# The rounding of a weight unit moved from ahead of a projection's successor to right behind the projection

## The chip, the cores and the metric

The kernel runs on one core of a Trainium2 chip. Its time is device microseconds of that core. Three runs of the kernel before took 1092.4 to 1093.69 us, median 1093.59.

The core's engines work side by side, each through its own list of instructions in order: TensorE (PE in the profile; its weight loads are PEld), VectorE (DVE), ScalarE (ACT), GpSimd (POOL) and SyncE (SP, which here only starts transfers). They wait for each other through semaphores.

## The reference

Batch 1, 256 positions, width 1024, float32. One block of three mixers and two more layers:

```python
h = rms_norm(x, norm1_g[l]);  u = h @ w_in[l]        # 1024 -> D_IN
(dq, dk, dv, iq, ik, iw, nq, nkv, ng, sz, sxbc, sdt, mg) = jnp.split(u, offsets, axis=-1)
y_a = dsa_mixer(...)     # indexed attention, 16 heads
y_b = nsa_mixer(...)     # compressed, selected and window attention, 16 heads
y_c = ssd_mixer(...)     # state space mixer: causal conv, scan by chunks, norm
mix = g0 * (y_a @ w_br_dsa[l]) + g1 * (y_b @ w_br_nsa[l]) + g2 * (y_c @ w_br_ssd[l])
x = x + mix @ w_out[l]
x = x + jnp.square(jax.nn.relu(rms_norm(x, norm2_g[l]) @ w_ff1[l])) @ w_ff2[l]
```

Then an even layer (`even_mixer`: a gated, 31-tap convolved and layer-normed half `ya`, and a multi-scale pooled half `yb`, joined by an output projection), an odd layer (`odd_mixer`: a 4-tap convolution, two gates by small per-head products, a linear recurrence over time, a gate, an output projection), each added to x, and a last norm. Everything is a matrix product of a normed activation by a weight, and elementwise work and recurrences around it.

## The kernel before

**Weights.** All projection weights come as one stream of 286 units of 512 KB (eight blocks of 128 x 128 float32), in the order in which they are used, into a ring of five places (`RING`, SyncE, from L603). Products are made in a split form: a weight W is rounded to fp32r, W_hi, and the rest, W_lo = W - W_hi, is kept beside it; so is each activation. For each block TensorE makes three products of 128 x 256: W_hi by x_hi, W_hi by x_lo, W_lo by x_hi (L1794, L1795, L1796). The weights of `b_val` and `pool` (`PLAIN`) are taken in one product (L1779), without splitting; the other 276 units are split.

**A step `wsplit`** of unit u is two instructions. ScalarE writes W_hi into one of three places (`ring_hi`, `HIS` = 3; L897), when the transfer has landed and TensorE is through with the split unit three before (L896). GpSimd or VectorE then subtracts (`remainder`, L562): the function `on_gpsimd` gives 182 units to GpSimd (all of dq, nq, br_dsa, val_glu, b_gate, a_gate, even_yb, xr, gate, two in three of xbc, half of others) and 94 to VectorE. TensorE waits for the remainder before a unit's first block.

**Jobs.** A job is one output block of 128 channels of one projection: `PHASES` lists each projection with its number of jobs and the blocks in each. Most have 8 blocks, one unit a job; `pool` has 2, `odd_out` 12, `br_ssd` 16, `ff2` 32. A job writes one of three PSUM slots and its reader frees it.

**Order.** `schedule()` writes one list of steps by hand, and each engine walks this list in order and issues its share of every step. There is no planner. A job step is TensorE's matmuls and, on ScalarE or VectorE, the reading of its PSUM slot (L981 on, L1007, L1012, L1030). Behind a job stand the steps that go with it; here they are called its epilogue: `split` (rounding L918 or L920 and remainder L570 or L1140 of a finished activation, for a later projection), `sA` to `sR` (softmax), `xconv` (L1361, the convolution, which frees the PSUM slot of xbc), `uA`, `uE`, `uB`, `ysq`, `ysum` (state space), `econv` (L1432), `winsum` (L731 to L735, on GpSimd), `gact`, `scan` and others. For the eight jobs of the head (`HEAD`: iq twice, ik, dk, kc, vc, ks, kw) and the first six of val_glu (`LATE`), the input's norm is not known when TensorE starts; ScalarE reads their slots only when VectorE has scaled them in place (step `scale`, L1147), a step behind the next job.

The `wsplit` of unit u stands directly ahead of the job in which unit u-2 begins (`AHEAD` = 2). Between two jobs a and b the list thus reads: job a, a's epilogue, `wsplit` of the unit two ahead, job b. Places that come up below: br_dsa 0 reads the split outputs of the DSA attention, whose last `split` steps stand behind mg 23; even_yb 0 reads the splits of yb, behind the last pool jobs; even_ya 0 reads those of ya, behind even_yb 7.

The code around the change, with what calls it:

Of the kernel before, what the change touches and what calls it, by code (L numbers as in the profile page):

```python
# [40 lines left out]
for _name, _w in COLUMNS:  # L41
# [5 lines left out]
PHASES = [("iq", 2, 8), ("ik", 1, 8), ("dk", 1, 8), ("kc", 1, 8), ("vc", 1, 8), ("ks", 1, 8), ("kw", 1, 8),  # L47
          ("dq", 8, 8), ("nq", 8, 8), ("xbc", 24, 8), ("sz", 16, 8), ("mg", 24, 8),
          ("br_dsa", 8, 8), ("br_nsa", 8, 8), ("br_ssd", 8, 16), ("w_out", 8, 8),
          ("ff1", 32, 8), ("ff2", 8, 32), ("val_glu", 16, 8), ("b_val", 8, 8), ("b_gate", 8, 8),  # L50
          ("a_gate", 8, 8), ("pool", 8, 2), ("even_yb", 8, 8), ("even_ya", 8, 8), ("xr", 12, 8), ("gate", 12, 8),
          ("odd_out", 8, 12)]
# [38 lines left out]
def schedule():  # L91
# [128 lines left out]
    order = first + a_gate + jobs["b_gate"] + pool  # L220
# [71 lines left out]
    at, splits = 0, {}  # L292
    order = [s for s in out if s[0] == "job"]
# [4 lines left out]
    for u in range(units):  # L298
        if starts[8 * u][1] not in PLAIN:
            splits.setdefault(("units", u) if u < AHEAD else starts[8 * (u - AHEAD)], []).append(("wsplit", u))  # L300
    final = []
    for s in out:
        final += splits.get(s, []) + [s]
    out = final
    assert len(set(out)) == len(out)
    return out
# [44 lines left out]

def program(nc, x_t, w_stream, w_tok, w_cmp, w_rgi, cols, rows, out):
    steps = schedule()
    where, turns = psum_tenants(steps)
    slots = {"proj": 3, "score": 2, "turn": 1, "pv": 1, "mean": 1}
# [1523 lines left out]
```

How the kernel before makes its waits and increments, by code:

```python
        def readers_done(eng, key):  # L502
            g, n = where[key]
            prev = n - slots[g]
            if prev >= 0:
                for e in turns[g][prev]:
                    eng.wait_ge(read[g, e], sum(e in r for r in turns[g][:prev + 1]))
# [1 line left out]
        def was_read(eng, key, reader="A"):  # L510
            g, n = where[key]
            eng.wait_ge(read[g, reader], sum(reader in r for r in turns[g][:n + 1]))
# [45 lines left out]
        def remainder(eng, u):  # L559
            eng.wait_ge(sem("w_hi_ready"), hi_turn[u])
            return eng.tensor_tensor(ring_lo[:, u % RING, :, :].rearrange("p k n -> p (k n)"),
                                     ring[:, u % RING, :, :].rearrange("p k n -> p (k n)"),
                                     ring_hi[:, hi_slot[u], :, :].rearrange("p k n -> p (k n)").bitcast(F32),
                                     ALU.subtract)
# [1 line left out]
        def part_remainder(eng, tag, c):  # L567
            src, hi, lo, _, _ = parts[tag]
            eng.wait_ge(sem(f"hi_{tag}"), c + 1)
            return eng.tensor_tensor(lo(c), src(c), hi(c).bitcast(F32), ALU.subtract)
# [21 lines left out]
        @block.sync  # L592
# [8 lines left out]
                    sp_eng.dma_start(wcmp, w_cmp).then_inc(sem("wcmp_in"), 16)  # L601
                if u >= RING:
                    sp_eng.wait_ge(filled["proj"], used[u - RING])
                if u == first["job", "even_ya", 5] // 8:
                    sp_eng.wait_ge(sem("yaf_ready"), 8)
                    sp_eng.dma_start(flat(WG, 12), w_rgi).then_inc(sem("wrgi_in"), 16)
```

## Time and profile before

| | |
|---|---|
| median of three runs | 1093.59 us (1092.4 to 1093.69) |
| the profiled execution | 1093.34 us |
| its span, first instruction to last | 1091.6 us, 21399 instructions |
| TensorE busy | 1050.3 us, 96%, 8185 matmuls |
| VectorE, ScalarE, GpSimd busy | 704.0, 594.9, 602.4 us |
| HBM read | 155.65 MB |

1.7 us of the profiled execution lie around its span. All times in the rows are microseconds from the start of the span, except where a row says ns. A busy time counts an engine as busy from the start of an instruction to its end; for TensorE neighbouring matmuls overlap, so their mean is longer than their spacing.

### The profile page before, as it was taken

The page shows a single profiled execution, that of the slowest core. Times are in us where ns is not written, and L with a number is a line of the kernel's source. Part 1 is how long each engine was busy: PE and PEld are TensorE (multiplying, and loading weights), DVE is VectorE, ACT ScalarE, POOL GpSimd, SP SyncE. Part 2 cuts the span into 40 slices and gives each one's busy share as a digit, 9 for nine tenths or more (in the row PEclk, how much of TensorE's full clock was granted, in tenths as well). Part 3 has the DMA queues.
Part 4 walks back from the last instruction along what each step waited for, and adds up shares of the span by engine and source line. Part 5 has one row for each costly group of instructions (what it writes and reads, how often), then busy time and mean ns, then how long its engine had stood idle before and what let it go on. Part 6 is the DMA issues. An engine that isn't in the chain of part 4 may idle for free.

```text
span 1091.6 us, 21399 instructions
## 1 busy us (share of the span) xinstructions
PE 1050.3 (96%) x8185; PEld 986.2 (90%) x8185; DVE 704.0 (64%) x1479; ACT 594.9 (54%) x1193; POOL 602.4 (55%) x454
## 2 busy tenths in 40 slices
PE   9999999999999999999999999999999989999986
PEld 8799878998889999889999999999898978899986
DVE  7869676666663325785485553333898967588974
ACT  5454667667664457764445554335333447368742
POOL 3656445444444469545534334337678857466951
PEclk9999999999999999999999999999999999999999
DMA  8234333333224443225545555555444534544442
GB/s 314 96 123 143 117 104 110 116 117 116 97 98 136 136 135 98 97 97 175 183 164 177 190 177 187 180 175 174 155 157 145 182 125 145 194 138 153 152 144 72
DMA packets 43157, 158.08 MB, mean 145 GB/s; under 512 B 4912, under 2 KB 4912, under 8 KB 42672
## 3 DMA queue, kind: packets, MB, share of 16 engines
q1 hardware_dynamic: 42912, 156.69, 43.0%
q8 instruction: 65, 1.06, 0.4%
q14 instruction: 36, 0.29, 0.1%
q10 hardware_dynamic: 144, 0.03, 0.0%
HBM read 155.65 MB, written 1.05 MB: 144 GB/s over the span
## 4 chain that ended last, share of the span: by engine, by line
PE 75%; DVE 14%; ACT 5%; POOL 3%; issue 2%; DMA 0%; DVEq 0%; SPq 0%; ACTq 0%; POOLq 0%
PE p_proj L1794 20%; PE p_proj L1795 19%; PE p_proj L1796 19%; PE p_score L1632 3%; PE p_proj L1779 3%; PE p_pv L1660 2%; POOL ring_lo L562 2%; ACT ring_hi L897 1%; PE p_turn L1642 1%; DVE ring_lo L562 1%; PE p_mean L1541 1%; PE p_score L1552 1%; DVE arena L1361 1%; PE p_score L1700 1%; POOL arena_r L570 1%
## 5 line engine op out<-in xcount | busy, mean ns | idle before, releaser
L1794 PE MATMUL p_proj<-arena_r,ring_hi 128*128 128x256 f32 x2208 | 657.7, 298 | 15.7 <-POOL ring_lo L562 6.5
L1795 PE MATMUL p_proj<-arena_r,ring_hi 128*128 128x256 f32 x2208 | 625.6, 283 | 0.0
L1796 PE MATMUL p_proj<-arena_r,ring_lo 128*128 128x256 f32 x2208 | 625.5, 283 | 0.0
L562 POOL TENSOR_TENSOR ring_lo<-ring,ring_hi 128x1024 fp32r<-128x1024 f32 x182 | 437.8, 2407 | 287.5 <-ACT ring_hi L897 286.7
L1794 PEld LDWEIGHTS p_proj<-arena_r,ring_hi 128*128 128x128 f32 x2208 | 423.7, 192 | 35.1 <-issue 19.9
L1795 PEld LDWEIGHTS p_proj<-arena_r,ring_hi 128*128 128x128 f32 x2208 | 424.2, 192 | 8.1 <-issue 6.0
L1796 PEld LDWEIGHTS p_proj<-arena_r,ring_lo 128*128 128x128 f32 x2208 | 423.9, 192 | 0.0
L897 ACT ACTIVATE ring_hi<-ring 128x1024 fp32r<-128x1024 f32 x276 | 290.3, 1053 | 108.0 <-PE p_proj L1796 105.1
L562 DVE TENSOR_TENSOR ring_lo<-ring,ring_hi 128x1024 fp32r<-128x1024 f32 x94 | 118.2, 1257 | 67.4 <-ACT ring_hi L897 65.9
L671 POOL TENSOR_TENSOR sbuf_s<-sbuf_s,srow 128x256 f32<-128x256 f32 (+1 forms) x48 | 41.8, 870 | 83.5 <-DVE srow L1343 58.2
L920 ACT ACTIVATE arena_r<-arena 128x256 fp32r<-128x256 f32 x108 | 42.4, 409 | 46.1 <-DVE arena L1511 22.3
L570 POOL TENSOR_TENSOR arena_r<-arena,arena_r 128x256 fp32r<-128x256 f32 x61 | 49.5, 824 | 18.0 <-ACT arena_r L920 18.0
L918 ACT ACTIVATE arena_r<-arena,par 128x256 fp32r<-128x256 f32 x48 | 23.7, 505 | 63.1 <-DVE arena L1518 49.8
L1518 DVE TENSOR_TENSOR arena<-arena,p_proj 128x256 f32<-128x256 f32 x40 | 16.8, 421 | 63.3 <-PE p_proj L1796 62.3
L1331 DVE CUSTOM_DVE_ANT_0 sbuf_s<-p_score,caus,nrq 128x128 f32<-128x128 f32 (+1 forms) x64 | 24.2, 415 | 41.0 <-PE p_score L1632 40.8
L1030 ACT ACTIVATE th<-p_proj 128x256 f32<-128x256 f32 x44 | 16.8, 383 | 58.6 <-PE p_proj L1796 58.6
L1432 DVE SCALAR_TENSOR_TENSOR p_score<-arena,par,p_score 128x256 f32<-128x256 f32 x116 | 46.9, 482 | 1.2
L843 ACT ACTIVATE sbuf_s<-sbuf_s,srow 128x128 f32<-128x128 f32 (+1 forms) x96 | 42.6, 450 | 3.7 <-DVE srow L1331 3.7
L1779 PE MATMUL p_proj<-arena,ring 128*128 128x256 f32 x160 | 38.3, 393 | 4.5 <-issue 2.4
L1779 PEld LDWEIGHTS p_proj<-arena,ring 128*128 128x128 f32 x160 | 30.7, 197 | 9.7 <-issue 2.4
L570 DVE TENSOR_TENSOR arena_r<-arena,arena_r 128x256 fp32r<-128x256 f32 x47 | 28.4, 605 | 15.3 <-ACT arena_r L920 13.8
L1154 DVE SCALAR_TENSOR_TENSOR arena<-p_proj,rinv 128x256 f32<-128x256 f32 x32 | 13.6, 424 | 37.3 <-PE p_proj L1796 37.2
(283 smaller groups left out, 1187.6 us busy)
## 6 DMA issues: line engine op xcount, KB each, us to landing
ring<-w_stream SPq DMA_DIRECT2D x286, 512.0 KB, 3.3
arena<-w_tok SPq DMA_DIRECT2D x1, 1632.0 KB, 13.0
arena<-w_rgi SPq DMA_DIRECT2D x1, 1536.0 KB, 6.5
arena<-x_t SPq DMA_DIRECT2D x4, 256.0 KB, 6.7
arena<-w_cmp SPq DMA_DIRECT2D x1, 1024.0 KB, 15.7
out_t<-arena SPq DMA_DIRECT2D x4, 256.0 KB, 2.6
par<-cols SPq DMA_DIRECT2D x1, 323.0 KB, 3.1
row<-rows ACTq DMA_DIRECT2D x1, 32.0 KB, 3.3
```

Source lines behind the costliest of these rows:

```text
L562: return eng.tensor_tensor(ring_lo[:, u % RING, :, :].rearrange("p k n -> p (k n)"), ring[:, u % RING, :, :].rearrange("p k n -> p (k n)") ...
L570: return eng.tensor_tensor(lo(c), src(c), hi(c).bitcast(F32), ALU.subtract)
L671: pool.tensor_tensor(p, p, r.unsqueeze(2).to_broadcast([P, 2, kl]), ALU.mult)\
L843: ins = act.activation(p, p, ACT.Exp, bias=srow[:, i % 4, 2 + h:3 + h], scale=-1.0, accum_out=srow[:, i % 4, 4 + h:5 + h])
L897: act.activation(ring_hi[:, hi_slot[u], :, :].rearrange("p k n -> p (k n)"), ring[:, u % RING, :, :].rearrange("p k n -> p (k n)"), ACT.Copy)\
L920: ins = act.activation(hi(c), src(c), ACT.Copy)
L1432: ins = dve.scalar_tensor_tensor(out=A(AC + cc) if tap == CONV_K - 1 else acc, in0=ub[:, cc, tap:tap + S], scalar=col("even_cw", CONV_K * ...
L1632: pe.matmul(ps, A(q + c)[:, P * t:P * t + P], kk[:, :, 0:kl], start=True, stop=True)\
L1779: mm = pe.matmul(slot(s)[:, 0:S], ring[:, u % RING, b % 8, :], rhs[c], start=(c == 0), stop=(c == n - 1))
L1794: pe.matmul(slot(s)[:, 0:S], w_hi, hi, start=(c == 0), stop=False)
L1795: pe.matmul(slot(s)[:, 0:S], w_hi, lo, start=False, stop=False)
L1796: mm = pe.matmul(slot(s)[:, 0:S], w_lo, hi, start=False, stop=(c == n - 1))
```

## The change

The tail of `schedule()` places the `wsplit` steps. For two consecutive jobs a and b that both have at most eight blocks, what stood directly ahead of b now stands directly behind a, that is, ahead of a's epilogue. Where either has more (br_ssd, ff2, odd_out) nothing is moved. Each step is still issued once, on the same engines; SyncE's list of transfers is the same.

```diff
@@ -298,9 +298,14 @@
     for u in range(units):
         if starts[8 * u][1] not in PLAIN:
             splits.setdefault(("units", u) if u < AHEAD else starts[8 * (u - AHEAD)], []).append(("wsplit", u))
+    size = {name: k for name, _, k in PHASES}
+    behind = {}
+    for a, b in zip(order, order[1:]):
+        if size[a[1]] <= 8 and size[b[1]] <= 8 and b in splits:
+            behind[a] = splits.pop(b)
     final = []
     for s in out:
-        final += splits.get(s, []) + [s]
+        final += splits.get(s, []) + [s] + behind.get(s, [])
     out = final
```

## Rows read from the trace of the kernel before

**Rows 1.** The page, part 4: the chain that ended last, by engine.

```profile
PE 75%; DVE 14%; ACT 5%; POOL 3%; issue 2%; DMA 0%; DVEq 0%; SPq 0%; ACTq 0%; POOLq 0%
```

**Rows 2.** The page, part 5, remainders and rounding: busy, mean ns | idle before, releaser.

```profile
L562 POOL TENSOR_TENSOR ring_lo<-ring,ring_hi 128x1024 fp32r<-128x1024 f32 x182 | 437.8, 2407 | 287.5 <-ACT ring_hi L897 286.7
...
L897 ACT ACTIVATE ring_hi<-ring 128x1024 fp32r<-128x1024 f32 x276 | 290.3, 1053 | 108.0 <-PE p_proj L1796 105.1
L562 DVE TENSOR_TENSOR ring_lo<-ring,ring_hi 128x1024 fp32r<-128x1024 f32 x94 | 118.2, 1257 | 67.4 <-ACT ring_hi L897 65.9
```

**Rows 3.** Windows: PE, PEld, DVE, ACT, POOL busy (instructions); granted clock, DMA share, GB/s.

```profile
450.00:500.00 50.00, 47.60 (x404) 44.17 (x403) 41.40 (x65) 30.75 (x63) 27.54 (x16) 1.00 0.35 114
600.00:650.00 50.00, 50.00 (x419) 50.00 (x419) 26.25 (x44) 29.47 (x54) 19.76 (x10) 1.00 0.56 183
...
900.00:950.00 50.00, 45.73 (x346) 44.58 (x345) 32.67 (x62) 28.41 (x47) 29.38 (x18) 0.97 0.51 170
```

**Rows 4.** Timeline of the head: start, duration, instruction [idle before it, releaser].

```profile
25.90 1.54 ACT L995 ACTIVATE arena<-p_proj 32x256 f32<-32x256 f32 x4
...
22.94 1.22 DVE L562 TENSOR_TENSOR ring_lo<-ring,ring_hi 128x1024 fp32r<-128x1024 f32 x1 [0.23 <-ACT ring_hi L897]
...
28.61 0.36 PE L1794 MATMUL p_proj<-arena_r,ring_hi 128*128 128x256 f32 x1 [0.24 <-POOL ring_lo L562]
```

**Rows 5.** Timeline of VectorE and TensorE at an xbc job.

```profile
209.11 1.52 DVE L1361 SCALAR_TENSOR_TENSOR arena<-p_proj,half,arena 128x253 f32<-128x253 f32 x3
...
211.87 0.47 PE L1794 MATMUL p_proj<-arena_r,ring_hi 128*128 128x256 f32 x1
```

**Rows 6.** Timeline of GpSimd and TensorE at br_dsa 0.

```profile
410.80 1.80 POOL L570 TENSOR_TENSOR arena_r<-arena,arena_r 128x256 fp32r<-128x256 f32 x2
412.56 2.37 POOL L562 TENSOR_TENSOR ring_lo<-ring,ring_hi 128x1024 fp32r<-128x1024 f32 x1
...
411.18 0.38 PE L1794 MATMUL p_proj<-arena_r,ring_hi 128*128 128x256 f32 x1 [0.59 <-DVE arena_r L570]
```

**Rows 7.** One line's instructions, L1511: duration in ns, min/median/max, first and last start.

```profile
L1511 DVE TENSOR_TENSOR arena<-arena,sqb x16: 424/479/2603, 458.3 to 538.6; 128x256 f32<-128x256 f32 x16
```

**Rows 8.** Timeline of GpSimd and TensorE at the squares of y.

```profile
473.64 2.39 POOL L562 TENSOR_TENSOR ring_lo<-ring,ring_hi 128x1024 fp32r<-128x1024 f32 x1 [1.23 <-ACT ring_hi L897]
...
477.54 0.45 PE L1714 MATMUL p_pv<-sbuf_s,arena 128*64 128x128 f32 x4 [0.50 <-DVE arena L1402]
...
484.30 1.40 PE L1726 MATMUL p_mean<-th,mean_d 128*128 128x256 f32 x4 [1.65 <-ACT th L950]
```

**Rows 9.** Timeline of GpSimd and TensorE behind the last window sum.

```profile
830.99 7.02 POOL L562 TENSOR_TENSOR ring_lo<-ring,ring_hi 128x1024 fp32r<-128x1024 f32 x3
...
833.48 0.36 PE L1794 MATMUL p_proj<-arena_r,ring_hi 128*128 128x256 f32 x1 [1.88 <-POOL ring_lo L562]
```

**Rows 10.** Timeline of GpSimd at the last splits of yb.

```profile
893.79 4.20 POOL L570 TENSOR_TENSOR arena_r<-arena,arena_r 128x256 fp32r<-128x256 f32 x6
897.95 2.37 POOL L562 TENSOR_TENSOR ring_lo<-ring,ring_hi 128x1024 fp32r<-128x1024 f32 x1
```

**Rows 11.** Timeline of GpSimd and TensorE at the last split of ya.

```profile
926.21 2.35 POOL L562 TENSOR_TENSOR ring_lo<-ring,ring_hi 128x1024 fp32r<-128x1024 f32 x1 [0.21 <-ACT ring_hi L897]
928.52 1.70 POOL L570 TENSOR_TENSOR arena_r<-arena,arena_r 128x256 fp32r<-128x256 f32 x1
...
930.28 0.52 PE L1794 MATMUL p_proj<-arena_r,ring_hi 128*128 128x256 f32 x1 [3.60 <-POOL arena_r L570]
```

**Rows 12.** Windows of 4 us behind two stalls, columns as in rows 3.

```profile
834.00:838.00 4.00, 4.00 (x24) 4.00 (x23) 1.99 (x5) 0.08 (x1) 4.00 (x2) 0.60 0.00 0
...
930.00:934.00 4.00, 3.72 (x18) 3.73 (x19) 1.33 (x3) 1.46 (x2) 0.90 (x2) 0.57 0.50 127
```

**Rows 13.** Timeline of GpSimd in the gate stretch.

```profile
1025.61 2.41 POOL L562 TENSOR_TENSOR ring_lo<-ring,ring_hi 128x1024 fp32r<-128x1024 f32 x1
1027.98 0.91 POOL L570 TENSOR_TENSOR arena_r<-arena,arena_r 128x256 fp32r<-128x256 f32 x1
```

## Prediction

> **What bounds the kernel now.** I read the chain that ended last first: TensorE holds 75% of the span and the rest is spread over waits for VectorE (14%), ScalarE (5%) and GpSimd (3%) [rows 1]. Then the costliest groups, for the two steps that the change moves. A rounding takes ScalarE 1.05 us (276 of them), a remainder 2.41 us on GpSimd (182) or 1.26 on VectorE (94). Two things stand in the releaser column: before a rounding ScalarE idled 108.0 us, 105.1 of it for TensorE, and before remainders GpSimd idled 287.5 us, nearly all for a rounding [rows 2]. So both steps mostly run as early as their waits allow, and seldom bound TensorE themselves. The windows say where the rest is lost: 50.00 of 50 us busy in ff1, but 47.60 from 450 to 500 and 45.73 from 900 to 950 [rows 3]. Those stretches decide, each with its own chain.
>
> **What the change can move at all.** Nothing is added or removed, and SyncE's transfers keep their order. The rounding of unit u waits for TensorE to have finished unit u-3 (three slots). The units stand two ahead of their jobs, so the job "a" behind which the rounding now stands is the very one that uses u-3 where a job is one unit: the rounding can start no earlier than a's last matmul. What changes is who goes first on three in-order engines once a has ended: before, a's epilogue steps (evictions, softmax and convolution steps, splits), then rounding and remainder; after, rounding and remainder first. Each moved unit can thus gain up to the epilogue's length for its remainder, and costs the epilogue 1.05 us on ScalarE, and on the engine of the remainder that engine's wait for the rounding besides its 2.41 or 1.26: 3.5 us on GpSimd, 2.3 on VectorE, counted from a's end [rows 2], where that engine has nothing older to do. Where TensorE is saturated (ff1, 490 to 770) both orders leave it busy: cost 0; a split or eviction put back by 3.5 us would still have the job two ahead as cover. If that cover were gone it would show as a drop from 50.00 in the ff1 window.
>
> **Part by part** (plus is slower; the sum is against the profiled execution, 1093.34 us, its 1091.6 us span and 1.7 around it; the median shown, 1093.59, is 0.25 above it).
> 1. Head, 12 to 50 us. A head job's own eviction is a step behind its successor, so it now stands behind a rounding. ik's four-part eviction takes 1.54 us [rows 4] and vc needs its slot (three PSUM slots): rounding 1.05, then 1.54, then fixed costs between engines put vc some 1.6 us late (estimate). VectorE's remainder of unit 4 (1.22, now at 22.94) moves ahead of the first scaling, and dk, which needs that slot, loses some 1.2. What goes are the stall behind a GpSimd remainder at 28.61, 0.24 us idle (0.5 with the start of the matmul), and half of a like one at 35. 1.6 + 1.2 - 0.5 = +2.3; bounds +1.7 and +3.0 (0.6 either way for the places that I can't read).
> 2. 115 to 330 us, softmax and xbc. A third of the remainders here are VectorE's, and each now stands with its wait ahead of the softmax steps and the three convolution steps (1.52 us) that free a PSUM slot. The one at 209.11 ends at 210.63 and TensorE enters the slot at 211.87 [rows 5]: 1.24 us of cover. Of the 2.3 us that the remainder takes from a's end I estimate that 1.5 reach the slot, so 0.3 is lost at each of four such places before 252, 1.2 in all; later the softmax groups leave a delay of some 0.7, under that cover. To this come one slot near 178 that has no cover, 0.85 (the remainder's 1.26 less VectorE's idle time), and 0.5 each at two places where a double softmax group goes behind the rounding (half of its 1.05); at 130 a chain gains 0.3. Estimates all: 1.2 + 0.85 + 1.0 - 0.3 = +2.8; bounds 0 (everything under cover) and +5 (every one of the four loses the whole 1.26).
> 3. 404 to 413 us, br_dsa 0 behind mg 23. It waits for the splits of the DSA output. Now GpSimd's remainder (2.37, from 412.56) stands behind the last two splits, and TensorE, which idled 0.59 for a split, starts at 411.18 [rows 6]. Afterwards the remainder is ahead of them, and the idle time grows by nearly the whole of it: +2.3; bounds 0 and +3.4 (rounding too). Near 443, where one rounding goes ahead of an exponential that TensorE waits for, I estimate +0.65 of its 1.05.
> 4. 465 to 489 us, the other sign. The roundings of units 101 to 104 now stand behind the squares of y, which wait for VectorE. VectorE's addition L1511 takes 0.48 us in the median and once 2.60 [rows 7]: that one runs beside the remainder that starts at 473.64 on GpSimd; TensorE then idles 0.50 at 477.54 and 1.65 at 484.30 [rows 8]. With the rounding directly behind its job the remainder is over some 4 us earlier, the addition is short, and VectorE's chain no longer waits for the late rounding of 102. I take both stalls and the two of about 0.5 behind them as gone: -3.5; bounds -3.9 and 0.
> 5. 770 to 886 us. Three remainders stand behind a window sum on GpSimd, 7.02 us in one piece, and TensorE idles 1.88 for them [rows 9]. They go ahead; but a remainder two units on is then behind the window sum. I estimate two new stalls, 1.7 and 2.0 (most of one 2.41), against this one (1.88, with the start of the next matmul 2.3), the dip of the clock behind it (1.6, below), and two smaller ones of 1.4 together: 3.7 - 5.3 = -1.6, of which VectorE's convolution, which sets much of this stretch, takes back 0.5. -1.1; bounds -2.3 and +0.5.
> 6. 888 to 900 us, even_yb 0. One remainder stands ahead of the last six splits of yb and one behind them [rows 10]; then both stand ahead. The splits, for which TensorE waits, end 2.37 later, with the gap to an older remainder 2.7, and the layer norm's chain starts behind that job: +2.7; bounds 0 and +3.5.
> 7. 918 to 935 us, even_ya 0. Here the remainder (2.35) stands ahead of the last split of ya (1.70, as against 0.91 for such a split [rows 13], since VectorE works beside it), and TensorE idles 3.60 [rows 11]. After the change that remainder goes behind an earlier job and the last split ends some 3.1 earlier. -3.1, and with the dip of the clock (1.6 of the 1.7 below) -4.7; bounds -5.5 and 0.
> 8. 960 to 1047, xr and gate. GpSimd is full here, a remainder of 2.41 and a split of 0.91 per unit [rows 13], so order alone gains at most one unit once: -0.7; bounds -1.5 and 0. w_out to ff1: +0.2.
>
> The clock. The mean granted clock was 0.60 from 834 to 838 and 0.57 from 930 to 934, part of it at the lower of the two levels (1.2 GHz), each time right behind the stall of part 5 or 7 [rows 12]. Four us at these means have 4 x 0.40 = 1.6 and 4 x 0.43 = 1.7 us less of full clock. I take both dips as gone.
>
> The Trainium skill (TensorE: Matmul & The Clock Gate, Part 1: The HAM clock gate) has the array at half rate behind a stretch of idleness; the trace agrees for these two, while the window with the stall of 1.65 us at 484 shows 1.00 [rows 3, 8]. By that rule the new stalls of parts 5 and 6 may dip themselves, and the total would be up to 3.4 above mine (two times 1.7).
>
> Sum: 2.3 + 2.8 + 2.3 + 0.65 - 3.5 - 1.1 + 2.7 - 4.7 - 0.7 + 0.2 = +0.95. 1093.34 + 0.95 = 1094.3, and 0.25 for the median: **1094.5 us**, no change that a measurement of this kernel can tell (that takes about 0.2%, 2.2 us).
>
> Beside part 4 stands a rule of the Trainium skill (SBUF — State Buffer, SBUF: two separate sides): VectorE with two SBUF inputs and GpSimd lock each other out for a whole instruction. The 2.60 us beside a remainder that starts at 473.64 agrees [rows 7, 8]. It speaks against counting a moved remainder as pure gain: the lock moves with it, and by the rule alone part 4 would give back up to 2.2 us (2.60 less 0.42) at another addition.
>
> **Rivals.**
> A. Slower: the remainder takes the place of the split. Place: the hand-overs where the next job reads what the epilogue writes (parts 1, 3, 6). Price: 2.3 + 2.3 + 2.7 = 7.3, which holds since each stands on the chain that TensorE waits for. It decides if parts 4 and 7 bring less than half of their 8.2: then 7.3 + 3.65 (parts 2 and 443, w_out) - 4.1 - 1.8 = +5.0, 1098.6 us. For it: the orders are certain, while the gains hang on chains through two engines. Against it: the 3.60 at 930 is the longest stall shown, and the remainder ahead of the split is plainly in its chain [rows 11].
> B. Faster: the softmax part has more slack than I read (part 2 at 0) and part 3 half its price, since GpSimd could finish its remainder while TensorE still works at the scores, and the gate stretch gains its bound: 0.95 - 2.8 - 1.15 - 0.8 - 1.0 (part 5 at -2.1) = -4.8, 1088.8 us. For it: GpSimd's 287.5 us of idleness before remainders [rows 2] say that a remainder meets an empty engine more often than a full one.
> C. The move does nothing: the rounding waits for TensorE in both orders (105.1 us [rows 2]), and everything is hidden: 1093.6 us. Against it: the named rows have the remainder and the split in the order that the move turns round.
>
> **Chances.** Forecast 0.35 (own range 1092 to 1097), A 0.33, B 0.24, C 0.08. Range: A with one new dip (1.7) and part 1 at its bound (0.7) is 1101.0; B with parts 4 and 7 at theirs (0.4 and 0.8) is 1087.6: 1087.6 to 1101.0. Faster by over 0.2%: most of B and a tail, 0.28. Slower: A and the upper part of the forecast, 0.37. Within: 0.35.
>
> **What would show it.** Step 1: in the changed trace ik's eviction ends later than a rounding, and TensorE idles over 1 us before vc. Step 3: br_dsa's first matmul waits 2 to 3 us. Step 4: no idle over 0.5 us between 475 and 490. Step 6: the six yb splits start behind two remainders. Step 7: the 3.60 us idle is under 1 us and the clock there 1.00. The ff1 window stays at 50.00. The forecast is wrong if 115 to 330 loses more than 5 us, since I read its slack slot by slot and one chain through VectorE could add up, or if new clock dips appear.

## The result, and the profile after

Four runs of each kernel: 1119.84 us median with the change (1119.52 to 1120.34), 1093.47 before (1092.4 to 1093.69). The ratio is 1.0238, 95% interval 1.0224 to 1.0251: 26.4 us slower, where 1.0 was forecast and 7.5 was the end of the range. The profiled execution of the changed kernel took 1119.9 us, span 1118.2. All medians leave out two executions that took several times as long as the others of their kernel, one of e4 (5729.8 us) and one of e5 (3550.8 us, the one profiled, so of e5 only the times are used).

The page of the changed kernel answers to [rows 1, 2] like this (five lines of code were added, so lines of the kernel behind `schedule()` are five higher: L562 is L567, L897 is L902, L570 is L575):

```profile
PE 78%; DVE 11%; ACT 4%; issue 3%; POOL 3%; DMA 1%; SPq 0%; DVEq 0%; ACTq 0%; POOLq 0%
...
L567 POOL TENSOR_TENSOR ring_lo<-ring,ring_hi 128x1024 fp32r<-128x1024 f32 x182 | 437.1, 2403 | 367.5 <-ACT ring_hi L902 367.0
...
L902 ACT ACTIVATE ring_hi<-ring 128x1024 fp32r<-128x1024 f32 x276 | 290.9, 1055 | 179.2 <-PE p_proj L1801 175.9
L567 DVE TENSOR_TENSOR ring_lo<-ring,ring_hi 128x1024 fp32r<-128x1024 f32 x94 | 117.5, 1250 | 101.4 <-ACT ring_hi L902 100.6
...
L575 DVE TENSOR_TENSOR arena_r<-arena,arena_r 128x256 fp32r<-128x256 f32 x47 | 56.3, 1198 | 32.9 <-ACT arena_r L925 32.1
```

The change did what it says: ScalarE now waits 175.9 us for TensorE ahead of roundings (105.1 before), that is, it more often stands ready at the job's end, and GpSimd waits 367.0 instead of 286.7 for roundings. The moved operations take what they took. What is new is the last line: a split's remainder on VectorE, 128x256, takes 1.20 us in the mean. Before, the same 47 operations had this row:

```profile
L570 DVE TENSOR_TENSOR arena_r<-arena,arena_r 128x256 fp32r<-128x256 f32 x47 | 28.4, 605 | 15.3 <-ACT arena_r L920 13.8
```

VectorE's busy time rose from 704.0 to 757.0 us with not one instruction added. The windows, as in [rows 3] (TensorE, its weight loads, VectorE, ScalarE, GpSimd busy; then the granted clock):

```profile
50.00:100.00 50.00, 45.82 (x375) 43.37 (x374) 38.46 (x56) 21.52 (x46) 22.24 (x10) 0.97 0.32 104
...
450.00:500.00 50.00, 48.33 (x431) 44.17 (x430) 41.98 (x77) 38.18 (x90) 32.22 (x22) 1.00 0.29 96
...
600.00:650.00 50.00, 50.00 (x419) 50.00 (x418) 39.96 (x45) 29.01 (x52) 20.37 (x9) 1.00 0.54 181
...
900.00:950.00 50.00, 43.61 (x268) 39.48 (x266) 31.92 (x67) 30.45 (x55) 33.70 (x25) 0.90 0.35 117
```

ff1 (600 to 650) is as full as before, though VectorE is busy 40.0 instead of 26.3 us there: its operations are stretched, and nobody waits for them. To see where time is lost I set the first weight load of each job in one trace against the same in the other. That gives the delay so far, and its growth by stretch:

| stretch (times of before) | forecast, us | measured, us |
|---|---|---|
| head, to kw | +2.3 | +3.0 |
| 50 to 115, dq and nq | 0, not looked at | +5.2 |
| 115 to 330, xbc and softmax | +2.8 | +6.0 |
| 330 to 404, sz 10 | 0 | +1.5 |
| 404 to 450, br_dsa | +2.95 | +3.2 |
| 465 to 489, br_nsa | -3.5 | -2.4 |
| 490 to 760, w_out, ff | +0.2 | +2.0 |
| 760 to 886 | -1.1 | +0.1 |
| even_yb | +2.7 | +3.7 |
| even_ya | -4.7 | +0.3 |
| xr, gate, to odd_out 2 | -0.7 | +4.0 |

The clock took a part. The mean granted clock is 0.981 of full, 0.993 before: 0.019 x 1118.2 = 21.2 us of clock missing against 0.007 x 1091.6 = 7.6. Windows of 4 us over the whole span show eleven dips of 1.7 us, some of them running together, where the kernel before has three (at 834, 886 and 930). How many dips an execution has also differs among executions of one kernel: 16 of the kernel before, taken beside e1, have mean clocks of 0.988 to 0.993 and take 1097.0 to 1092.1 us, the lower the clock the longer. A single trace is therefore good to a dip or two, here some 2 to 3 us. Four of these windows, as in [rows 12]:

```profile
76.00:80.00 4.00, 4.00 (x23) 4.00 (x23) 0.66 (x5) 0.17 (x1) 0.00 (x0) 0.57 0.02 4
124.00:128.00 4.00, 4.00 (x21) 4.00 (x22) 1.07 (x4) 3.21 (x10) 0.00 (x0) 0.58 0.01 4
...
916.00:920.00 4.00, 3.22 (x12) 3.04 (x13) 0.42 (x1) 0.73 (x1) 2.10 (x4) 0.50 0.00 0
...
952.00:956.00 4.00, 4.00 (x21) 4.00 (x21) 2.92 (x3) 1.24 (x2) 2.42 (x1) 0.50 0.81 283
```

**The largest single loss, read closely.** At dq 4 the delay grows by 3.0 us, and by 1.5 more within the job, in the dip at 76. The timeline of the changed kernel there, GpSimd, VectorE and TensorE:

```profile
64.70 2.40 POOL L567 TENSOR_TENSOR ring_lo<-ring,ring_hi 128x1024 fp32r<-128x1024 f32 x1 [4.70 <-ACT ring_hi L902]
...
65.00 2.18 DVE L1267 TENSOR_SCALAR arena<-arena,tok 128x128 f32<-128x128 f32 x1 [3.24 <-ACT arena L819]
...
67.65 1.75 DVE L1239 RECIPROCAL rinv<-root 128x256 f32<-128x256 f32 x1
69.44 5.57 DVE L1251 SCALAR_TENSOR_TENSOR kk_w<-arena,half,rinv 64x256 f32<-64x256 f32 x4
...
75.42 0.41 PE L1584 MATMUL p_pv<-th,mean_h 128*128 128x64 f32 x2 [4.08 <-DVE th L1234]
```

and the same place before:

```profile
61.17 0.29 DVE L1262 TENSOR_SCALAR arena<-arena,tok 128x128 f32<-128x128 f32 x1 [5.50 <-ACT arena L814]
...
69.22 0.41 PE L1579 MATMUL p_pv<-th,mean_h 128*128 128x64 f32 x2 [1.09 <-DVE th L1229]
```

A scaling of 128 columns starts 0.30 us behind the remainder and ends 0.08 us behind it: 2.18 us for 0.29. Everything behind it on VectorE is late, and TensorE idles 4.08 us instead of 1.09. Of the 3.0 us, 1.9 are this operation, 0.5 the four at L1251 (5.57 us for 5.09), and 0.6 order alone: the eviction that the scaling waits for now stands behind a rounding on ScalarE, so the scaling starts 3.83 us later than before, in a kernel that was 3.21 late there.

### The profile page after: what moved, and what is told of

The parts are those of the page before. It is cut to its first block, busy times and chain, and to the rows that moved or that the text cites. A ratio compares the mean times of both kernels' runs of the same rounds, so it can differ in the third digit from the quotient of the medians.

```text
span 1118.2 us, 21409 instructions
## 1 busy us (share of the span) xinstructions
PE 1062.4 (95%) x8185; PEld 996.6 (89%) x8185; DVE 757.0 (68%) x1479; ACT 591.8 (53%) x1193; POOL 594.3 (53%) x454
## 3 DMA queue, kind: packets, MB, share of 16 engines
HBM read 155.65 MB, written 1.05 MB: 140 GB/s over the span
## 4 chain that ended last, share of the span: by engine, by line
PE 78%; DVE 11%; ACT 4%; issue 3%; POOL 3%; DMA 1%; SPq 0%; DVEq 0%; ACTq 0%; POOLq 0%
PE p_proj L1799 21%; PE p_proj L1800 20%; PE p_proj L1801 20%; PE p_score L1637 3%; PE p_proj L1784 2%; PE p_pv L1665 2%; ACT ring_hi L902 2%; POOL ring_lo L567 2%; PE p_turn L1647 1%; DVE ring_lo L567 1%; DVE arena_r L1145 1%; PE p_mean L1546 1%; PE p_score L1557 1%; PE p_score L1755 1%; PE p_score L1705 1%
## 5 line engine op out<-in xcount | busy, mean ns | idle before, releaser
L567 POOL TENSOR_TENSOR ring_lo<-ring,ring_hi 128x1024 fp32r<-128x1024 f32 x182 | 437.1, 2403 | 367.5 <-ACT ring_hi L902 367.0
L1799 PEld LDWEIGHTS p_proj<-arena_r,ring_hi 128*128 128x128 f32 x2208 | 428.0, 194 | 40.1 <-issue 21.0
L1800 PEld LDWEIGHTS p_proj<-arena_r,ring_hi 128*128 128x128 f32 x2208 | 428.5, 194 | 8.4 <-issue 6.2
L1801 PEld LDWEIGHTS p_proj<-arena_r,ring_lo 128*128 128x128 f32 x2208 | 428.2, 194 | 0.0
L902 ACT ACTIVATE ring_hi<-ring 128x1024 fp32r<-128x1024 f32 x276 | 290.9, 1055 | 179.2 <-PE p_proj L1801 175.9
L567 DVE TENSOR_TENSOR ring_lo<-ring,ring_hi 128x1024 fp32r<-128x1024 f32 x94 | 117.5, 1250 | 101.4 <-ACT ring_hi L902 100.6
L575 DVE TENSOR_TENSOR arena_r<-arena,arena_r 128x256 fp32r<-128x256 f32 x47 | 56.3, 1198 | 32.9 <-ACT arena_r L925 32.1
L575 POOL TENSOR_TENSOR arena_r<-arena,arena_r 128x256 fp32r<-128x256 f32 x61 | 49.3, 823 | 13.5 <-ACT arena_r L925 13.5
L1145 DVE SCALAR_TENSOR_TENSOR arena_r<-arena,par,arena_r 128x256 fp32r<-128x256 f32 x48 | 43.5, 906 | 8.1 <-ACT arena_r L923 5.8
L1494 DVE SCALAR_TENSOR_TENSOR arena<-th,p_proj 128x256 f32<-128x256 f32 x44 | 18.5, 422 | 34.2 <-ACT th L1035 32.7
```

Of the source, the lines that this page charges most:

```text
L567: return eng.tensor_tensor(ring_lo[:, u % RING, :, :].rearrange("p k n -> p (k n)"), ring[:, u % RING, :, :].rearrange("p k n -> p (k n)") ...
L575: return eng.tensor_tensor(lo(c), src(c), hi(c).bitcast(F32), ALU.subtract)
L902: act.activation(ring_hi[:, hi_slot[u], :, :].rearrange("p k n -> p (k n)"), ring[:, u % RING, :, :].rearrange("p k n -> p (k n)"), ACT.Copy)\
L1145: dve.scalar_tensor_tensor(out=lo(c), in0=src(c), scalar=col(GAIN[tag], c), in1=hi(c).bitcast(F32), op0=ALU.mult, op1=ALU.subtract)\
L1799: pe.matmul(slot(s)[:, 0:S], w_hi, hi, start=(c == 0), stop=False)
L1800: pe.matmul(slot(s)[:, 0:S], w_hi, lo, start=False, stop=False)
```

## The experiments

**The rounding alone (e1).** The remainder keeps its old place in the list of VectorE and GpSimd.

```diff
-                elif k == "wsplit" and on_gpsimd(s[1]):      # and so on VectorE
+                elif k == "wrest" and on_gpsimd(s[1]):
-        final += splits.get(s, []) + [s] + behind.get(s, [])
+        rest = [("wrest", x[1]) for x in stay.get(s, [])]   # stay: the old places
+        final += splits.get(s, []) + rest + [s] + behind.get(s, [])
```

> Only the rounding on ScalarE stands directly behind the job; the remainder stays where the kernel before has it, on both engines. Theory L (port lock: GpSimd's remainder now starts just ahead of VectorE's epilogue operations and holds them up; stretched VectorE operations are where the loss begins): the remainders start behind the epilogue again on GpSimd's and VectorE's lists, so the addition L570, the multiplication L1343 and L1140 keep their short times and the time is near the kernel before, 1090 to 1098 us. Rival Q (queue order on ScalarE: 1.05 us of rounding ahead of exponentials, evictions and roundings of activations is what TensorE waits for): most of the 26.4 us stays, 1110 us or more.

1112.0 us, ratio 1.017 (1.0153 to 1.0187), which is rival Q's range. My expectation for theory L failed, but not the lock: VectorE, then TensorE in that trace (its lines are six higher than before):

```profile
62.80 2.17 DVE L1268 TENSOR_SCALAR arena<-arena,tok 128x128 f32<-128x128 f32 x1 [3.98 <-ACT arena L820]
...
73.21 0.66 PE L1585 MATMUL p_pv<-th,mean_h 128*128 128x64 f32 x2 [4.07 <-DVE th L1235]
```

The operation is as long as in the changed kernel, and VectorE is busy 742.1 us in all (704.0 before, 757.0 changed). GpSimd's place in the list hardly mattered here, since it had nothing else to do: the rounding's end starts the remainder. This run can't tell ScalarE's order from the lock; for that the lock must go.

**Fills in place of GpSimd's remainders (e2, e3, e9).** The same edit on three orders: changed, before, rounding alone.

```diff
-                    remainder(pool, s[1]).then_inc(...)
+                    pool.wait_ge(sem("w_hi_ready"), hi_turn[s[1]])
+                    spot = ring_lo[...]                      # the same 1024 columns
+                    link(pool.memset(spot, 0.0))
+                    link(pool.memset(spot, 0.0))
+                    pool.memset(spot[:, 0:256], 0.0).then_inc(...)
```

> The changed kernel, where GpSimd writes zeros (two fills of 1024 and one of 256 columns, some 2.2 us together, estimated from the 0.30 us of 240 columns) instead of subtracting: the weights' remainders that GpSimd makes are left out, its place in the order and its waits stay, but it no longer reads SBUF. Theory L: VectorE's stretched operations fall back to their short times (L570 from 1.20 us mean towards 0.6, L1343 to 0.16) and most of the loss goes: at or under 1100 us. Rival Q (order in the queues alone): within 5 us of 1119.8.

> The kernel before with the same replacement, as the other end of the comparison: what the lock costs in the old order. Theory L: 3 to 8 us less than 1093.5, since the long operations L1511 (2.60 us) and the last split of ya are stretched there too. Rival Q: within 2 us of 1093.5.

> As the run with the rounding alone moved, and GpSimd again writes zeros in place of its remainders (those are left out), so that no VectorE operation is locked out by them. It is to be set against the kernel before with the same fills, 1081.4 us. Theory L1 (of the 18.5 us of the rounding alone, most is the lock, since GpSimd idles for the rounding and starts the moment it is done, wherever its step stands): 1082 to 1087 us. Rival S (ScalarE's 1.05 us ahead of its epilogue steps costs by itself): 1092 us or more.

The three fills take 0.95, 0.95 and 0.31 us, from the first's start to the last's end some 2.34, so GpSimd is held as long as by a remainder of 2.40. Medians in us:

| GpSimd makes | before | rounding moved | both moved |
|---|---|---|---|
| remainders | 1093.5 | 1112.0 | 1119.8 |
| fills, reading nothing | 1081.4 | 1086.6 | 1097.3 |
| difference | 12.1 | 25.4 | 22.5 |

Ratios to the kernel before: 1.0029 (1.0013 to 1.0045) for e2, 0.9884 (0.9859 to 0.9908) for e3, 0.9938 (0.9923 to 0.9953) for e9. In e2 the long operations are short; from its page and its timeline at dq 4:

```profile
L575 DVE TENSOR_TENSOR arena_r<-arena,arena_r 128x256 fp32r<-128x256 f32 x47 | 21.1, 449 | 34.8 <-ACT arena_r L929 34.1
```

```profile
63.21 0.71 DVE L1271 TENSOR_SCALAR arena<-arena,tok 128x128 f32<-128x128 f32 x1 [7.08 <-ACT arena L823]
```

and no wait of TensorE at that place is left. VectorE is busy 645.0 us in e3, 648.2 in e9 and 644.7 in e2: with fills, the order no longer changes how long its operations take. So: moving the rounding costs 5.2 us by order (1086.6 - 1081.4) and 13.3 more by the lock (18.5 - 5.2); moving the remainder too costs 10.7 by order, and no more lock (7.8 in all). Of the 26.4 us, 15.9 are order and 10.5 the lock that the order brings about. By the intervals of e2 and e3 both parts are good to some 3 us only: e2's ten executions lie between 1093.8 and 1101.2. Of e9's two theories L1 held (1082 to 1087). Theory L's number for e2 held too, and its 3 to 8 us for e3 was too small. But the order's part is the larger one, which only rival Q had named.

The fills do not take the whole lock away, against what e9's expectation says. The scaling takes 0.71 us in e2, not 0.29: GpSimd's first fill starts 0.32 us ahead of it, and the scaling again ends 0.08 us behind it. The two-input operations that follow run beside the other fills and are short, four in 1.97 us (5.57 in the changed kernel):

```profile
62.89 0.95 POOL L715 MEMSET ring_lo<- 128x1024 f32 x1 [4.58 <-ACT ring_hi L906]
...
66.18 1.97 DVE L1255 SCALAR_TENSOR_TENSOR kk_w<-arena,half,rinv 64x256 f32<-64x256 f32 x4
```

GpSimd's remainders of activations (L570) also stay in all three. A small part of the lock may thus stand in the order's part.

**By the engine of the remainder (e5, e6).** Units moved only where GpSimd, or only where VectorE, makes the remainder: one more condition, e.g. `and not any(gp[x[1]] for x in splits[b])`.

> Only the units whose remainder GpSimd makes are moved, those of VectorE stay ahead of the next job. Theory L+Q (of the 26.4 us some 10.5 to 12.8 are VectorE operations locked out by GpSimd's remainders that now start beside them, and some 14 to 16 the order in the queues): the lock part comes whole and the order part by the larger share of the units, together 1108 to 1116 us. Rival V (what costs is VectorE, whose list is held by a remainder that waits for its rounding ahead of convolution and softmax steps): 1096 to 1102 us.

> The reverse of the run before: only units whose remainder VectorE makes are moved. Theory L+Q: 1095 to 1102 us (no new lock). Rival V: most of the loss, 1112 us or more.

1121.6 us, ratio 1.0257 (1.0236 to 1.0279), and 1105.6, ratio 1.011 (1.0072 to 1.0148). Both are above what theory L+Q expected and far from rival V. They do not add either, 28.8 and 12.7 to 26.4; my reading, not tested, is that a list in which one unit's steps stand early and the next one's late has both orders' costs. e6's four executions fall in two pairs, 1102.0 and 1102.4 at clocks of 0.992 and 0.990, and 1108.7 and 1109.8 at 0.986. In e6 the head alone cost 4.0 us by kw, in e1 0.1: what the head loses is VectorE's remainder ahead of `scale`, not the rounding ahead of ik's eviction.

**By stretch (e4, e10, e12, e13).** The condition in the loop gets `b[1] == "br_nsa"`; or b from br_nsa 0 on; or br_nsa and the units 212, 214, 241, 243; or `b[1] != "dq"`.

> Only the units that stood ahead of the br_nsa jobs are moved, the stretch in which TensorE gained 2.7 us on the kernel before by the job starts (from +19.25 to +16.45 us). If stretches add up: 1090.8 us, 2.7 under the kernel before. Rival: the gain there was only the slack that the earlier loss had given to SyncE's transfers and to older remainders, and alone it brings nothing, 1093.5.

1090.5 us, ratio 0.9967 (0.9951 to 0.9982), 3.0 us under the kernel before: the gain of part 4 is real and stands alone. L1511 (here L1516) had 2603 ns as its longest in [rows 7], now:

```profile
L1516 DVE TENSOR_TENSOR arena<-arena,sqb x16: 424/480/1523, 460.1 to 538.2; 128x256 f32<-128x256 f32 x16
```

> Only the units ahead of br_nsa 0 and later are moved; everything to 450 us is as before. By the starts of the jobs in the changed kernel (19.25 us late at br_nsa 4, 16.45 at br_nsa 7, 25.8 at odd_out 1) stretches that add up give -2.7 + 9.3 = +6.6: 1100 us. Rival (the later losses exist only because the first half shifted the hand-overs and the clock's dips): within 2 us of 1091, the time of br_nsa alone.

1100.7 us, ratio 1.0072 (1.0051 to 1.0093): stretches add up, so the other 19 us belong to the first 450 us.

> br_nsa's units and four others are moved, 212 and 214 (behind the window sums) and 241 and 243 (ahead of the last splits of ya), whose stalls got shorter in the changed kernel. Theory (a move pays only where a remainder was what TensorE waited for): the stalls of 0.5 to 2.3 us at 817 to 833 shrink by 2 us and that at 930 by 2 to 3, 1086 to 1088 us. Rival (each such move makes the lock or a new stall as large): 1091 us or more.

1092.8 us, ratio 0.9994 (0.9985 to 1.0004): the rival. The stalls at 817 and 824 went (the delay falls by 0.5 and 0.9) and val_glu 15 lost 1.9 in exchange, 1.54 of it a wait for a GpSimd remainder; what even_ya had gained, 5 us in hand at xr 0, was down to 0.2 at the end of xr 1.

> The changed kernel, with the eight units that stood ahead of the dq jobs (10 to 17) put back. Theory L (the largest single loss of the first half, 2.98 us at dq 4 and 1.5 of clock behind it, is the lock: L1262 takes 2.18 us instead of 0.29 beside a remainder that starts 0.30 us ahead of it, and the four L1246 and the reciprocal behind it follow): that operation is short again, TensorE idles near 1.1 instead of 4.1 us ahead of the matmul at L1579, and the time is 4 to 6 us less than the changed kernel, 1114 to 1116 us. Rival (what is saved there is lost at the next hand-over, mg 0 at 124 us): 1118 us or more.

1112.7 us, ratio 1.017 (1.0148 to 1.0192), 7.2 us under the changed kernel, more than the 4.5 that the place itself had shown. TensorE's wait is back at its old size:

```profile
71.86 0.41 PE L1584 MATMUL p_pv<-th,mean_h 128*128 128x64 f32 x2 [1.10 <-DVE th L1234]
```

The trace has five dips instead of eleven: beside that at 76 those at 948 and 1072 us are gone, others are half as long, and one at 850 is new. The surplus over 4.5 may be such dips; the run does not tell.

**TensorE kept busy in its stalls (e7, e8, e11, e14).** Trains of matmuls with a constant, into the PSUM slot that the next matmul overwrites, ahead of a wait:

```diff
                     readers_done(pe, s)
+                    busy(s, idle.get(s, 0))   # e14: {("qsq", 3): 16}, 9 in even_yb 0, 4 in even_ya 0
                     pe.wait_ge(sem("qsq_ready"), i + 1)
```

> The changed kernel, with TensorE given idle matmuls of 128 columns in six of its stalls, each train shorter than the stall (30 ahead of the wait of 4.1 us at 75 us, the others 8 to 18), so that it is busy where it was idle. Theory C (each long stall also costs a dip of the granted clock, about 1.7 us, some 13.6 us of the 26.4 by the windows): the dips at 76, 916 to 922 and 948 to 956 us go, and 4 to 6 us with them, 1114 to 1116 us. Rival: the dips come with the waits themselves or what they cost is given back at the next wait, 1119.8 us or more.

> The kernel before, with such trains of idle matmuls in two stalls, 16 behind the window sums (a_gate 0) and 26 ahead of the last split of ya (even_ya 0). Theory C: the dips at 834 and 930 us go, 3.4 us less, 1090.1 us. Rival: as in the run before, 1093.5 us.

1119.4 us, ratio 1.0232 (1.021 to 1.0254), and 1099.0, ratio 1.005 (1.0034 to 1.0067), neither of them theory C's number. All trains were twice as long as meant, as each such matmul is two instructions of 0.114 us: 52 instructions took 5.96 us in e8, in a stall of 3.60. They say little of what a dip costs. In e7 the dips at 76 and between 916 and 956 went, five of the eleven, and the time stayed, with trains longer than the stalls they fill; in e8 two dips of the kernel before went and two new ones came at 408 and 960.

> The changed kernel with trains of idle matmuls of the right length: 32 instructions of 0.114 us (3.65 us, stall 4.08) at 75 us, 18 (2.05 us, stall 2.37) in even_yb 0 and 8 (0.9 us, stall 1.15) in even_ya 0. Theory C (a dip costs its loss of clock): three dips go, 4 to 5 us less, 1115 to 1116 us. Rival D (what TensorE gains it waits for at the next hand-over from VectorE, as the 3.3 us gained by 952 us with br_nsa's units, of which 0.3 was left at the end): 1118 to 1120 us.

With trains shorter than the stalls: 1115.1 us, ratio 1.0187 (1.0165 to 1.021), 4.8 under the changed kernel. The profiled execution took 1112.8 us at a clock of 0.993; the other three have 0.988 to 0.991 and took 1114.3 to 1116.4. In its trace the windows of the dips at 76 and 952 show:

```profile
76.00:80.00 4.00, 4.00 (x36) 4.00 (x35) 0.52 (x4) 1.52 (x3) 0.00 (x0) 1.00 0.14 38
...
952.00:956.00 4.00, 4.00 (x33) 3.81 (x32) 2.21 (x5) 1.28 (x2) 0.14 (x1) 1.00 0.98 399
```

> The kernel with br_nsa's units alone moved, and two trains of idle matmuls on TensorE, this time shorter than the stalls: 16 instructions of 0.114 us (1.8 us) at a_gate 0 and 26 (3.0 us, stall 3.6) ahead of the last split of ya. In the first try they were double and ended 1.5 and 2.2 us late. Theory C (a dip costs what the clock shows): the dips behind both stalls go, 1091.2 - 3.2 = 1088.0 us. Rival: new dips come elsewhere, as at 408 and 960 us in the first try, 1091 us or more.

1091.5 us, ratio 0.9977 (0.9965 to 0.9988), no better than e4 (1090.5), as the rival said. Both dips went and TensorE was 6.4 us ahead of the kernel before at xr 0. Then it waited for VectorE's chain of even_ya, which had not become faster, and dipped there:

```profile
954.73 0.58 PE L1812 MATMUL p_proj<-arena_r,ring_hi 128*128 128x256 f32 x1 [3.07 <-DVE arena_r L1145]
```

So the clock's share of the loss is real, but only where TensorE is the one that is late. In the changed kernel's trace 13.6 us more of clock are missing than before. The execution of e14 that had all of that back (0.993) was 7.1 us faster than the changed kernel's, and the median of the four, whose clocks average 0.990, was 4.8 us faster. And the changed kernel's own four executions differ by 0.8 us only, with clocks from 0.980 to 0.986, 6.7 us apart in clock time.

## Why the prediction was wrong

Forecast +1.0, measured +26.4.

**The step that failed first** is the cost of a moved unit, "1.05 us on ScalarE, and on the engine of the remainder that engine's wait ... besides its 2.41 or 1.26". It leaves out the third engine, VectorE beside GpSimd. A GpSimd remainder that starts at a's end starts just ahead of VectorE's epilogue operations of the same job, and holds up each that finds it running: 2.18 us for 0.29 at 65.0, 1.20 us in the mean for the 47 operations at L570. Before, the rounding stood behind the epilogue on ScalarE, and thereby kept the remainder clear of it. I had the rule of the Trainium skill beside part 4 (SBUF — State Buffer, SBUF: two separate sides), and wrote that "the lock moves with it", but sized it by one place, 2.2 us, where 207 units change their place, 144 of them with a remainder by GpSimd, and gave it neither a rival nor a chance. The same section of the Trainium skill also says that a GpSimd operation holds off VectorE operations in a two-port performance mode, not only those with two SBUF inputs, and that the latter are held off only by one that reads SBUF. The scaling at 65.0 has one tensor as input and was held off, by a remainder (2.18 us) and by a fill (0.71 us, e2), while two-input operations beside fills were not; this agrees, but no trace shows which mode an operation runs in. Measured, the lock's part is 10.5 us, with the dips that its long stalls set off. The larger part, 15.9 us, is order: the moved operations took as long as before, but places where they delay others were missing from the sum, or stood in it with too little or as a gain (below).

**The stretches at nothing.** 50 to 115 us had no term in the sum. TensorE was 48.9 of 50 us busy from 50 to 100 before, and the one stall, 1.09 us at 69.2, stood at the end of a long VectorE chain with no slack at all. It became the largest loss of one place. Putting the eight units of dq back gave 7.2 us. sz 10 had no term either: GpSimd's operation at L685 went behind a remainder, TensorE waited 1.23 us for it, and with fills in the same order it lost as much (1.4). w_out and ff had 0.2, since "both orders leave it busy", and lost 2.0. At w_out 2, where 1.4 of it fell, VectorE's operation beside a remainder is the lock once more, 0.43 us in the median; the three runs with fills lose nothing there:

```profile
558.79 2.56 DVE L1104 TENSOR_TENSOR arena<-arena 128x256 f32<-128x256 f32 x1
...
561.49 0.67 PE L1546 MATMUL p_mean<-arena,mean_d 128*128 128x256 f32 x2 [1.18 <-DVE arena L1104]
```

**Part 1** had its size (+3.0 for +2.3) and half of its reason: by e1 and e6 it is VectorE's remainder of units 4 and 6 ahead of `scale`, and TensorE then waits for ik's eviction, which itself is on time for its `scale`:

```profile
30.75 1.54 ACT L1000 ACTIVATE arena<-p_proj 32x256 f32<-32x256 f32 x4 [1.83 <-DVE p_proj L1152]
...
32.34 0.38 PE L1799 MATMUL p_proj<-arena_r,ring_hi 128*128 128x256 f32 x1 [1.70 <-ACT arena L1000]
```

**Part 2** was twice the estimate. Nor is it the lock: with fills (e2 against e3) the delay grows by 6.2 us from mg 1 to sz 0, by the starts of the jobs. (From mg 0 it is 4.7, as e3 lost 1.5 to a dip at 115 us that e2 does not have.) It is 1.7 at xbc 2, which I had not named, with a dip right behind it that makes 1.6 more of difference by mg 5; 1.0 at xbc 6, where I had 0.85; and 0.4 to 0.6 at each of four slots from xbc 12 to 17, where I had 0.3. The 0.3 was the difference of two numbers of 1.5 and 1.24, where a small error doubles the result.

**Part 3** had its size (+3.2 for +2.95) by luck. GpSimd was through with the remainder at 424.1 and did the last two splits at 428.09, so br_dsa's first matmul did not wait 2 to 3 us for them, it waited for nothing; that is what rival B had said. What grew are two waits one step earlier, 2.19 us for 1.44 behind an exponential on ScalarE and 1.05 for 0.23, and two dips came behind them. e14's trace has the same two waits (2.19 and 1.09) without a dip, and its delay grows by 2.0 there, not 3.2. The changed kernel:

```profile
423.36 1.20 PE L1705 MATMUL p_score<-upper,dta 128*128 128x128 f32 x8 [2.19 <-ACT sbuf_s L887]
425.61 1.12 PE L1719 MATMUL p_pv<-sbuf_s,arena 128*64 128x128 f32 x8 [1.05 <-DVE arena L1407]
...
421.57 2.53 POOL L567 TENSOR_TENSOR ring_lo<-ring,ring_hi 128x1024 fp32r<-128x1024 f32 x1
428.09 1.82 POOL L575 TENSOR_TENSOR arena_r<-arena,arena_r 128x256 fp32r<-128x256 f32 x2
```

**Part 4** held: -2.4 in the changed kernel and -3.0 (by e4's interval 2.0 to 5.4) for it alone, by the mechanism given. With fills instead of remainders there is nothing to gain there (e2 loses none and gains none against e3), which fits the lock as its cause.

**Part 6** held: the remainder now stands ahead of the last splits of yb. From pool 7 to even_yb 2 the delay grows by 4.3 us, with two dips behind the wait, and by 2.7 in e14, where neither comes.

```profile
913.70 2.35 POOL L567 TENSOR_TENSOR ring_lo<-ring,ring_hi 128x1024 fp32r<-128x1024 f32 x1
916.01 2.09 POOL L575 TENSOR_TENSOR arena_r<-arena,arena_r 128x256 fp32r<-128x256 f32 x3
...
916.78 0.58 PE L1799 MATMUL p_proj<-arena_r,ring_hi 128*128 128x256 f32 x1 [2.37 <-POOL arena_r L575]
```

**Part 7** failed. The 3.60 us of [rows 11] went, but the remainder that left the last split now stood ahead of the three before it, and two waits came in its place, with a dip behind them:

```profile
947.52 0.39 PE L1799 MATMUL p_proj<-arena_r,ring_hi 128*128 128x256 f32 x1 [0.77 <-POOL arena_r L575]
950.68 0.58 PE L1799 MATMUL p_proj<-arena_r,ring_hi 128*128 128x256 f32 x1 [1.15 <-POOL arena_r L575]
```

I had priced what the move takes away and not the next place on the same list, and e11 and e12 show that a gain there would have been given back at xr 0 in any case. **Parts 5 and 8**: 760 to 886 came out even. xr and gate lost 4.0 where I had -0.7. One wait there is new, 1.37 us for VectorE's convolution at 989 us, and 1.6 us of delay. The norm's root on ScalarE now stands behind a rounding that waits for the job's end (it starts at 981.88; then a table load of 1.28 us, then the root), and the convolution waits for the root. It is order, not the lock: e9, with fills and only the rounding moved, has the same wait of 1.37 and the same 1.6. The rest I have only as sums, and no run takes it apart.

**The clock.** I expected two dips to go. That at 834 went; at even_ya 0 the clock is low for twice as long as before (the window from 952 above), and the trace has eleven dips in place of three. That a long stall costs twice was in my text only as up to 3.4 us.

**Rival A** named the right side. Its mechanism (the remainder takes the split's place) is at most a part of the order's 15.9 us, where I had 11.0 for the places I knew: 5.2 of them come with the rounding alone, ahead of any moved remainder, and at br_dsa 0, one of its three places, it did not happen. What no single experiment separates is how the lock's 10.5 us divide between stretched operations and the dips behind them.

## What to carry to other kernels

Ahead of moving an operation between engines' lists, ask not only who waits for it, but who runs beside it at its new time, and on two engines that lock each other out count each pair that will overlap. A step behind an idle engine's wait has no place in the list: what releases it sets its time, so look at the releaser. A long stall of TensorE should be priced with the clock's dip behind it, but a gain only counts as far as the next hand-over at which the other engine is late; the only moved units that paid were the seven of br_nsa, among them the one remainder that had been shown beside a stretched operation in TensorE's chain. e12's four others, chosen the same way, paid nothing.

## What was not expected of the hardware

A fill by GpSimd (0.95 us for 1024 columns) left VectorE's two-input operations at 0.45 us in the mean beside it, where a subtraction of the same total length stretched them to 0.61 (before) and 1.20 us (changed). That single-input scaling was held off by a fill as well, 0.71 us for 0.29. The kernel before loses 12.1 us to GpSimd's subtractions already, four times what the best order tried here gains (e4, 3.0 us). TensorE's clock dips are not tied to a place: with their two stalls filled, two came elsewhere in the same kernel, and e4 dipped at 116 us behind a stall that both it and the kernel before have.
